# A decoder trunk whose expert search, weight splits and gate products are laid out again over the chunks of one weight stream

## The chip, the cores and the metric

One of the eight cores of a Trainium2 chip runs the whole kernel. The metric is the device time of one execution, in microseconds (us). TensorE (PE) multiplies, VectorE (DVE), ScalarE (ACT) and GpSimd (POOL) work element by element, SyncE (SP) issues transfers. Only TensorE writes products to PSUM, which has eight banks of 128 x 512 float32.

## The reference

Two layers act on `x`, 512 tokens of 1024 numbers. Each layer is a mixer (three kinds of attention) and then PEER, an expert layer, which the change is about:

```
def peer_ffn(xn, w_q, k1, k2, u, v):
    q = (xc @ w_q)                      # 8 heads, two halves of 128
    s1, s2 = q half . k1, q half . k2   # 128 scores each
    v1, i1 = lax.top_k(s1, 16);  v2, i2 = lax.top_k(s2, 16)
    cand = v1[..., :, None] + v2[..., None, :]      # 16 x 16 pairs
    top_s, top_pos = lax.top_k(cand, 16)
    ids = pair of key numbers of top_pos            # one of 128 * 128 experts
    g = jax.nn.softmax(top_s)
    act = u[ids] . xc
    y = sum over heads and 16 of  g * gelu(act) * v[ids]
```

So each token uses 8 x 16 of 16384 experts, each with a row of `u` and one of `v`.

## The kernel before, in words

All weights come as one stream of 1 MB chunks (128 x 2048 float32) through two buffers `raw[0]` and `raw[1]`. Each chunk is split for precision: ACT copies `raw` to `hi` in a rounded format (`split_hi`, L497, line L501), and DVE or POOL subtracts to get `lo` (`split_lo`, L833 on DVE with line L836; L459 on POOL with line L462). TensorE makes every product from three matmuls (`product`, L1323, lines L1325 to L1327): hi with hi, hi with lo, lo with hi. Semaphores `hi_done`, `lo_done` and `w_used` order the three: the hi split of a chunk waits until TensorE has used the chunk two before it.

PEER of a layer has these stages on TensorE:

- **Queries.** 8 chunks of `w_q`, one head each, and the key scores of that head. POOL makes the `lo` of these chunks.
- **U chunks.** 64 chunks of 256 experts. Instead of gathering rows, TensorE computes the activation of all experts for 352 of the 512 tokens: a chunk has two halves i = 0 and 1 (bank 0 and bank 1), each of 8 products, so 24 matmuls of 128x352 (`experts`, L1589). ACT applies Gelu to each bank (`gelu`, L694, lines L703 and L706), and `store_act` (L711) stores the result to DRAM.
- **Find.** Beside the first `FIND_STEPS` = 14 U chunks DVE does the search (L1081 to L1185): per head `top16` over both score halves, the candidate sums (L1106, L1108), `top16` over the candidates; then 15 rounds of a compare (L1150) and a predicated copy (L1153) over 1024 numbers that look the key numbers up. Between the rounds `low_half` makes the `lo` of chunks 9 to 14 (`LOW_HALF_AT`, L132); POOL makes that of chunks 2 to 8 in two halves (`HALVED`, line L480). In step 13 TensorE transposes the key numbers and gates of three tiles (L1611 to L1613, after waits for `idx_done` and `g_done`), and ACT evicts them (L736 to L738).
- **Gates.** For each of 352 tokens a 128 x 128 table of gates is made by one matmul of two one-hot matrices (`gates_of`, L1615, line L1623), four tokens to a group, 88 groups, one PSUM bank and one of four `onehot` slots (`G_RING`) per group. Beside each U chunk from 14 on TensorE makes three groups (`G_PER_STEP` = 3), one after half 0 and two after half 1, over 30 chunks. The one-hots of `idx1` (times the gate) are made by DVE for all groups (L1262, semaphore `oh_done`); those of `idx2` by DVE for the first group of a step (L1258) and by ACT for the other two (`OH_ACT`, `onehots`, L755: four squares, line L761, one per token, then one Relu over all four, line L764, semaphore `oh_act_done`). ACT evicts each group into `gate_s` (`g_evac`, L741, line L749) and stores eight groups as one 2 MB slice (`store_gates`, L751, line L753).
- **Tail.** The last 20 U chunks carry no gates.
- **Rows.** Tile 3 (128 tokens) and 32 tokens of tile 2 are done the sparse way: POOL gathers a row per token and rank (line L490), DVE multiplies and sums it (`row_op`, L1195; L1202 for the 32, L1204 for the 128). The 160 ops on `u` rows lie beside gates and tail.
- **V chunks.** 64 chunks; DVE multiplies activations and gates that SP loads back from DRAM (`weigh_step`), TensorE sums into all eight banks (`weighted`, L1650).

The order on each engine is written out by hand: an engine takes its instructions in order, and a wait holds all behind it. The ACT order in a gate step (L768 to L786) is what the prediction speaks of most:

```
ahead(lp + P_U + j, s)                     # hi split of the next chunk
for b in OH_ACT: onehots(...)              # two groups
gelu(0); g_evac; gelu(1); g_evac; store_act; g_evac
```

## Time and profile before

| | |
|---|---|
| median of 3 runs | 3315.04 us (3309.36 to 3315.66) |
| profiled execution | 3316.17 us |
| its span, first to last instruction | 3314.4 us |
| mean granted TensorE clock | 0.998 of 2.4 GHz |
| PE busy, DVE busy, ACT busy, POOL busy | 99%, 79%, 47%, 33% |

"Busy" is the time an engine executes. The time of an execution lies 1.8 us over its span. The two layers are alike; layer 0 ends at about 1650 us, and layer 1 repeats it some 1649 us later. The ends of matmuls are modelled, so the distance between two starts tells more than a busy share.

### The profile page before, as it was taken

The page shows a single profiled execution, that of the slowest core. Times are in us where ns is not written, and L with a number is a line of the kernel's source. Part 1 is how long each engine was busy: PE and PEld are TensorE (multiplying, and loading weights), DVE is VectorE, ACT ScalarE, POOL GpSimd, SP SyncE. Part 2 cuts the span into 40 slices and gives each one's busy share as a digit, 9 for nine tenths or more (in the row PEclk, how much of TensorE's full clock was granted, in tenths as well). Part 3 has the DMA queues.
Part 4 walks back from the last instruction along what each step waited for, and adds up shares of the span by engine and source line. Part 5 has one row for each costly group of instructions (what it writes and reads, how often), then busy time and mean ns, then how long its engine had stood idle before and what let it go on. Part 6 is the DMA issues. An engine that isn't in the chain of part 4 may idle for free. (4 is left out here: it accounts for less than half of the span.)

```text
span 3314.4 us, 55810 instructions
## 1 busy us (share of the span) xinstructions
PE 3269.3 (99%) x19734; PEld 3039.2 (92%) x19734; DVE 2610.5 (79%) x4992; ACT 1554.9 (47%) x2368; POOL 1087.6 (33%) x711
## 2 busy tenths in 40 slices
PE   8999999999999999999999999999999999999998
PEld 7767878999999999999987678789999999999998
DVE  6555448999997899999855644399999978999897
ACT  5554332467774333333355543334677733333333
POOL 1000003423335555555300000134333345555552
PEclk9999999999999999999999999999999999999999
DMA  4113322479999999999721133224899999999996
GB/s 146 62 52 115 140 104 81 171 286 383 379 383 389 420 403 411 403 409 410 284 90 64 42 124 140 103 82 176 310 379 382 378 404 416 402 409 407 404 405 251
DMA packets 230935, 894.83 MB, mean 270 GB/s; under 512 B 22784, under 2 KB 67984, under 8 KB 182912
## 3 DMA queue, kind: packets, MB, share of 16 engines
q1 hardware_dynamic: 116944, 465.34, 36.7%
q0 software_dynamic: 93008, 337.91, 26.1%
q10 hardware_dynamic: 20832, 89.74, 6.7%
q8 instruction: 72, 1.18, 0.1%
q14 instruction: 79, 0.65, 0.1%
HBM read 801.42 MB, written 91.49 MB: 269 GB/s over the span
## 5 line engine op out<-in xcount | busy, mean ns | idle before, releaser
L836 DVE TENSOR_TENSOR lo<-raw,hi 128x2048 fp32r<-128x2048 f32 (+1 forms) x320 | 728.9, 2278 | 287.4 <-ACT hi L501 284.9
L1325 PE MATMUL bank<-xT_hi,hi 128*128 128x352 f32 (+1 forms) x2688 | 928.7, 346 | 1.9 <-DVE xT_lo L886 1.7
L1326 PE MATMUL bank<-xT_lo,hi 128*128 128x352 f32 (+1 forms) x2688 | 911.5, 339 | 0.0
L1327 PE MATMUL bank<-xT_hi,lo 128*128 128x352 f32 (+1 forms) x2688 | 911.3, 339 | 0.0
L501 ACT ACTIVATE hi<-raw 128x2048 fp32r<-128x2048 f32 (+1 forms) x338 | 643.9, 1905 | 375.9 <-PE bank L1327 338.2
L1325 PE MATMUL bank<-w_hi,hi 128*128 128x352 f32 x2048 | 661.1, 323 | 0.5 <-DVE w_lo L1243 0.5
L1327 PE MATMUL bank<-w_hi,lo 128*128 128x352 f32 x2048 | 661.5, 323 | 0.0
L1326 PE MATMUL bank<-w_lo,hi 128*128 128x352 f32 x2048 | 658.1, 321 | 0.0
L1325 PEld LDWEIGHTS bank<-xT_hi,hi 128*128 128x128 f32 x2688 | 506.5, 188 | 32.3 <-issue 5.6
L490 POOL DMA_INDIRECT rows<-in_v_rows,ids x256 | 415.8, 1624 | 350.5 <-DVE h L1215 276.1
L1327 PEld LDWEIGHTS bank<-xT_hi,lo 128*128 128x128 f32 x2688 | 505.7, 188 | 26.0
L1326 PEld LDWEIGHTS bank<-xT_lo,hi 128*128 128x128 f32 x2688 | 507.2, 189 | 23.1
L490 POOL DMA_INDIRECT rows<-in_u_rows,ids x256 | 325.3, 1271 | 394.0 <-DVE act_row L1204 309.8
L1327 PEld LDWEIGHTS bank<-w_hi,lo 128*128 128x128 f32 x2048 | 386.7, 189 | 0.0
L1325 PEld LDWEIGHTS bank<-w_hi,hi 128*128 128x128 f32 x2048 | 384.4, 188 | 1.6 <-issue 1.0
L1326 PEld LDWEIGHTS bank<-w_lo,hi 128*128 128x128 f32 x2048 | 385.8, 188 | 0.0
L1215 DVE SCALAR_TENSOR_TENSOR h<-rows,w_row,h 128x1024 f32<-128x1024 f32 x256 | 327.6, 1280 | 7.3 <-DVE h L1215 1.4
L1204 DVE CUSTOM_DVE_ANT_0 rows<-rows,x_row 128x1024 f32<-128x1024 f32 x256 | 301.1, 1220 | 12.6 <-DMA rows<-in_u_rows,ids 12.6
L791 ACT ACTIVATE w_hi<-act_in 128x704 fp32r<-128x704 f32 x120 | 95.3, 794 | 392.2 <-DVE act_in L1238 392.2
L706 ACT ACTIVATE act_s<-bank 128x352 f32<-128x352 f32 x124 | 57.6, 465 | 278.3 <-PE bank L1327 278.3
L1262 DVE TENSOR_SCALAR onehot<-iota_sb,idx1T,gT 128x128 f32<-128x128 f32 x704 | 185.8, 356 | 1.0 <-ACT gT L738 1.0
L1623 PE MATMUL bank<-onehot 128*128 128x128 f32 x1408 | 176.0, 275 | 0.0
(227 smaller groups left out, 4254.1 us busy)
## 6 DMA issues: line engine op xcount, KB each, us to landing
raw<-in_stream SPq DMA_DIRECT2D x352, 1024.0 KB, 6.6
gate_d<-gate_s ACTq DMA_DIRECT2D x22, 2048.0 KB, 11.9
act_d<-act_s ACTq DMA_DIRECT2D x120, 352.0 KB, 6.4
act_in<-act_d SPq DMA_DIRECT2D x120, 352.0 KB, 7.0
gate_in<-gate_d SPq DMA_DIRECT2D x96, 384.0 KB, 9.6
gate_in<-gate_d SPq DMA_DIRECT2D x32, 256.0 KB, 4.8
rows<-in_u_rows,ids POOLq DMA_INDIRECT x256, 10.0
rows<-in_v_rows,ids POOLq DMA_INDIRECT x256, 7.5
```

What stands on the lines that cost most here:

```text
L490: pool.indirect_dma_start(rows[:, N % NR], None, a["u_rows" if n < U_ROW_OPS else "v_rows"], bass.IndirectOffsetOnAxis(which, 0)).then_inc ...
L501: act.activation(hi[s][:, 0:n], raw[s][:, 0:n], ACT.Copy).then_inc(hi_done, 1)
L706: act.activation(dst[:, s, 1, 0:TU], ps[1][:, 0:TU], ACT.Gelu).then_inc(gelu1, 1)
L791: act.activation(w_hi[:, s], acts_of(k, s), ACT.Copy).then_inc(w_hi_done, 1)
L836: dve.tensor_tensor(lo[s][:, 0:n], raw[s][:, 0:n], hi[s][:, 0:n].bitcast(F32), ALU.subtract).then_inc(lo_done, 1)
L1204: last = dve.tensor_tensor_reduce(row, row, x_row[:], 1.0, 0.0, ALU.mult, ALU.add, act_row[:, k])
L1215: last = dve.scalar_tensor_tensor(out=h[:, ROWED], in0=row, scalar=w_row[:, k], in1=h[:, ROWED], op0=ALU.mult, op1=ALU.add)
L1262: last = dve.tensor_scalar(o[:, r, 0], iota[:], idx1T[:, t], gT[:, t], ALU.is_equal, ALU.mult)
L1325: pe.matmul(dst, a_[0], b_[0], start=first, stop=False)
L1326: pe.matmul(dst, a_[0], b_[1], start=False, stop=False)
L1327: return pe.matmul(dst, a_[1], b_[0], start=False, stop=last)
L1623: last = pe.matmul(ps[4 + slot][:, tile(r)], o[:, 1], o[:, 0], start=True, stop=True)
```

## The change

`FIND_STEPS` goes from 14 to 10: the search must end four U chunks earlier. `G_PER_STEP` goes from 3 to 2: the 88 groups lie beside 44 chunks, one group after each half, and the tail shrinks from 20 chunks to 10. Of each four groups DVE makes the `idx2` one-hots of the last (`OH_DVE_AT` = 3), ACT those of the other three. Besides:

- the candidate sums move from DVE to POOL, with two buffers, and the pairs of a head are searched after the keys of the next head;
- the compare and copy of round a cover only ranks a to 15 of each 16;
- `low_half` makes the `lo` of chunks 9 and 10 alone. From chunk 11 on DVE makes the first half of each `lo`, POOL the second, between row gathers (`SHARED`, `second_half`);
- the row ops on `u` rows read their second operand from PSUM banks 2 and 3, into which ACT copies it twice per layer;
- the first V loads of gates start later (`GATES_AHEAD`), and the V blocks begin with banks 4 to 7.

The diff, cut to its core (`...` marks what is left out):

```
-FIND_STEPS = 14
-EXP_STEP, IDX_AT = 7, {13: (0, 1, 2)}
+FIND_STEPS = 10
+EXP_STEP, IDX_AT = 7, {9: (0, 1, 2)}
-G_RING, G_PER_STEP, G_TOK = 4, 3, 4
+G_RING, G_PER_STEP, G_TOK = 4, 2, 4
-V_BLOCKS = (2, 3, 4, 5, 6, 7, 0, 1)
+V_BLOCKS = (4, 5, 6, 7, 2, 3, 0, 1)
-E_GELU, E_WEIGH = 12, 14
-OH_ACT = (1, 2)
+E_GELU, E_WEIGH = 11, 13
+OH_DVE_AT = G_RING - 1
+OH_ACT = GROUPS - GROUPS // G_RING
+GATES_AHEAD = 2
...
-LOW_HALF_AT = (3, 5, 8, 10, 13)
+LOW_HALF_AT = (4,)
+CAND_AFTER = {3: 0, 4: 1, 5: 2, 7: 3, 8: 4, 9: 5, 11: 6, 12: 7}
...
@@ POOL
+                def candidates(hd):
+                    v, c = vals[:, hd % 2], cand[:, hd % 2]
+                    near, far = NEAR * TOPK, TOPK - NEAR
+                    pool.wait_ge(vals_done, PH * l + hd + 1)
+                    pool.tensor_tensor(c[:, :, 0:near]...)
+                    pool.tensor_tensor(c[:, :, near:]...).then_inc(cand_done, 1)
+                for n in range(1, C_WQ + 2):
+                    split_lo(lp + P_WQ + n // 2, n % 2)
+                    if n in CAND_AFTER:
+                        candidates(CAND_AFTER[n])
...
+                def second_half(c):
+                    s, half = c % 2, slice(HALF, CW)
+                    pool.wait_ge(lo0_done, LO0_PER_LAYER * l + len(HALVED) + c - FIND_STEPS)
+                    pool.tensor_tensor(lo[s][:, half], raw[s][:, half], hi[s][:, half].bitcast(F32),
+                                       ALU.subtract).then_inc(lo_done, 1)
+                for n in range(NR):
+                    fetch(n)
+                n = NR
+                for c in SHARED:
+                    second_half(c)
+                    while n < rows_by(c - SHARED.start) + NR:
+                        fetch(n)
+                        n += 1
@@ ACT, gate steps
                 for st in range(G_STEPS):
                     j, s = J_G + st // 2, st % 2
                     ahead(lp + P_U + j, s)
-                    for b in OH_ACT:
-                        if group(st, b) >= 0:
-                            onehots(group(st, b), OH_PER_LAYER * l + by_act(st, b))
+                    for b in range(G_PER_STEP):
+                        q = group(st, b)
+                        if q % G_RING != OH_DVE_AT:
+                            onehots(q, OH_ACT * l + by_act(q))
+                    if st == 0:
+                        act.wait_ge(e_link, 5 * l + 5)
+                        act.activation(x_in_ps, x_e, ACT.Copy).then_inc(x_ps_set, 1)
                     if st == E_GELU:
                         act.wait_ge(row_done, ROW_OPS * l + E)
+                        act.activation(x_in_ps, x_row[:], ACT.Copy).then_inc(x_ps_set, 1)
                         act.activation(w_e[:], act_e[:], ACT.Gelu).then_inc(e_gelu, 1)
                     for b in range(G_PER_STEP):
                         q = group(st, b)
-                        if b < 2:
-                            gelu(j, s, b)
-                        if q >= 0:
-                            g_evac(q)
+                        gelu(j, s, b)
+                        g_evac(q)
                         if b == 1:
                             store_act(j, s)
-                        if q >= 0 and q % PER_SLICE == PER_SLICE - 1:
+                        if q % PER_SLICE == PER_SLICE - 1:
                             store_gates(q // PER_SLICE)
@@ DVE, search
-                for hd in range(PH):
...
+                best_keys(0)
+                for hd in range(1, PH):
+                    best_keys(hd)
+                    best_pairs(hd - 1)
+                best_pairs(PH - 1)
...
-                        at[a] = looked(dve.tensor_scalar(chosen[a % 2], slot_f, float(a), None, ALU.is_equal))
+                        at[a] = looked(dve.tensor_scalar(by_rank(chosen[a % 2])[:, :, a:], by_rank(slot_f)[:, :, a:],
+                                                         float(a), None, ALU.is_equal))
...
@@ DVE, gate and tail steps
-                        if b not in OH_ACT:
+                        if q % G_RING == OH_DVE_AT:
...
-                    ahead(p, s)
+                    c = FIND_STEPS + st + 1
+                    if c in SHARED:
+                        dve.wait_ge(hi_done, 2 * (lp + P_U) + c + 1)
+                        half = slice(0, HALF)
+                        dve.tensor_tensor(lo[c % 2][:, half], ...).then_inc(lo0_done, 1)
@@ PE, gate steps
                     for i in range(2):
-                        experts(j if it is None else j + it * (G_RING // 2), s, i)
-                        for b in range(i, 2 * i + 1):
-                            q = group(st, b)
-                            if q >= 0:
-                                from_act = OH_PER_LAYER * l + 2 * ahead + by_act(st, b) if b in OH_ACT else None
-                                gates_of(l * GROUPS + G_PER_STEP * ahead + q, q % G_RING, from_act)
+                        experts(j if it is None else j + it * (G_RING // 2), s, i, shared=st > 0)
+                        gates_of(group(st, i), group(st, i) % G_RING, ahead)
```

What this does to the order of instructions is shown at three places; line numbers are those of each file (so the code of ACT's one-hots is L761 before and L807 now), `bank0` and `bank1` are the banks of the two halves, `bank4` to `bank7` those of the gate groups, and the words in brackets are the semaphores waited for.

TensorE in the second gate step, around the first group of the step; before:

```order
L1327 MATMUL bank0<-xT_hi,lo1 128x352
L1617 ISA
L1623 MATMUL bank5<-onehot 128x128 [waits g_ev,oh_done]
L1623 MATMUL bank5<-onehot 128x128 x3
L1325 MATMUL bank1<-xT_hi,hi1 128x352 [waits gelu1]
```

and now:

```order
L1394 MATMUL bank0<-xT_hi,lo1 128x352
L1686 ISA
L1688 ISA [waits oh_done]
L1692 MATMUL bank6<-onehot 128x128 [waits g_ev,oh_act_done]
L1692 MATMUL bank6<-onehot 128x128 x3
L1388 ISA
L1392 MATMUL bank1<-xT_hi,hi1 128x352 [waits gelu1,lo_done]
```

The group after half 0 waited for DVE's one-hots alone, and now waits for ACT's too (`oh_act_done`). The half behind it also waits for `lo_done` of its chunk.

ACT from the hi split of one gate step to that of the next; before:

```order
L501 ACTIVATE hi<-raw 128x2048 [waits w_used,raw_in1]
L761 ACTIVATE onehot<-iota_sb,idx2T 128x128 [waits g_ps]
L761 ACTIVATE onehot<-iota_sb,idx2T 128x128 x3
L764 ACTIVATE onehot<-onehot,one 128x4x128 [waits oh_act_link]
L761 ACTIVATE onehot<-iota_sb,idx2T 128x128 [waits g_ps]
L761 ACTIVATE onehot<-iota_sb,idx2T 128x128 x3
L764 ACTIVATE onehot<-onehot,one 128x4x128 [waits oh_act_link]
L703 ACTIVATE act_s<-bank 128x352 [waits act_out0,u0_ps]
L749 ACTIVATE gate_s<-bank 128x128x4 [waits g_ps]
L706 ACTIVATE act_s<-bank 128x352 [waits w_used]
L749 ACTIVATE gate_s<-bank 128x128x4 [waits g_ps]
L711 DMA act_d<-act_s 128x704 [waits gelu0,gelu1]
L749 ACTIVATE gate_s<-bank 128x128x4 [waits g_ps]
```

and now, in a step with an odd number (an even one has both groups' one-hots here); the last row but one stands in every fourth step:

```order
L547 ACTIVATE hi<-raw 128x2048 [waits w_used,raw_in0]
L807 ACTIVATE onehot<-iota_sb,idx2T 128x128 [waits g_ps]
L807 ACTIVATE onehot<-iota_sb,idx2T 128x128 x3
L810 ACTIVATE onehot<-onehot,one 128x4x128 [waits oh_act_link]
L749 ACTIVATE act_s<-bank 128x352 [waits act_out1,u0_ps]
L795 ACTIVATE gate_s<-bank 128x128x4 [waits g_ps]
L752 ACTIVATE act_s<-bank 128x352 [waits w_used]
L795 ACTIVATE gate_s<-bank 128x128x4 [waits g_ps]
L757 DMA act_d<-act_s 128x704 [waits gelu0,gelu1]
L799 DMA gate_d<-gate_s 128x4096 [waits g_ev]
L547 ACTIVATE hi<-raw 128x2048 [waits w_used,raw_in1]
```

The hi split stays in front of the one-hots, and the one-hots behind it are now those of the group after half 0 first.

DVE at the end of the search; before, the last rounds, with one of the five splits between rounds and the one behind them:

```order
L836 TENSOR_TENSOR lo1<-raw1,hi1 128x2048 [waits hi_done]
L1150 TENSOR_SCALAR rows<-rows 128x1024 [waits look_link]
L1153 COPY_PREDICATED rows<-rows,top_i 128x1024 [waits look_link]
L1150 TENSOR_SCALAR rows<-rows 128x1024 [waits look_link]
L1153 COPY_PREDICATED rows<-rows,top_i 128x1024 [waits look_link] x2
L836 TENSOR_TENSOR lo0<-raw0,hi0 128x2048 [waits hi_done]
L1161 TENSOR_REDUCE g_sum<-g_t 128x32 [waits exp_ready]
```

and now, from the split of chunk 9, behind which rounds 5 to 15 still stand:

```order
L1207 TENSOR_SCALAR rows<-rows 128x64x12 [waits look_link]
L1211 COPY_PREDICATED rows<-rows,top_i 128x64x13 [waits look_link]
L885 TENSOR_TENSOR lo1<-raw1,hi1 128x2048 [waits lo_done,hi_done]
L1207 TENSOR_SCALAR rows<-rows 128x64x11 [waits look_link]
L1211 COPY_PREDICATED rows<-rows,top_i 128x64x12 [waits look_link]
L1207 TENSOR_SCALAR rows<-rows 128x64x10 [waits look_link]
L1211 COPY_PREDICATED rows<-rows,top_i 128x64x11 [waits look_link]
```

Eleven compares (11 down to 1 rank wide) and twelve copies (12 down to 1) follow the split of chunk 9, then the split of chunk 10.

## Rows read from the trace of the kernel before

**Rows 1.** Windows, us: busy PE, PEld, DVE, ACT, POOL; PEclk; DMA share; GB/s.
```profile
850.00:900.00 50.00, 50.00 (x350) 50.00 (x349) 46.94 (x99) 38.92 (x79) 18.41 (x16) 1.00 0.95 371
1892.00:1902.00 10.00, 9.60 (x57) 6.32 (x57) 4.39 (x19) 5.20 (x18) 0.00 (x0) 0.83 0.01 2
```
**Rows 2.** Timeline of PE, one gate chunk and the next: start, us, operation.
```profile
807.38 0.41 PE L1325 MATMUL bank<-xT_hi,hi 128*128 128x352 f32 x1
...
811.30 1.05 PE L1623 MATMUL bank<-onehot 128*128 128x128 f32 x8
812.11 0.41 PE L1325 MATMUL bank<-xT_hi,hi 128*128 128x352 f32 x1
...
817.74 0.41 PE L1325 MATMUL bank<-xT_hi,hi 128*128 128x352 f32 x1
```
**Rows 3.** Timeline of ACT over the same chunk.
```profile
807.66 0.60 ACT L749 ACTIVATE gate_s<-bank 128x512 f32<-128x512 f32 x1 [0.30 <-PE bank L1623]
808.16 1.90 ACT L501 ACTIVATE hi<-raw 128x2048 fp32r<-128x2048 f32 x1
809.96 1.27 ACT L761 ACTIVATE onehot<-iota_sb,idx2T 128x128 f32<-128x128 f32 x4
811.26 0.72 ACT L764 ACTIVATE onehot<-onehot,one 128x512 f32<-128x512 f32 x1
...
814.16 0.59 ACT L749 ACTIVATE gate_s<-bank 128x512 f32<-128x512 f32 x1
814.78 0.34 ACTq L753 DMA_DIRECT2D gate_d<-gate_s  x1
```
**Rows 4.** Timeline of ACT, a find step: a DMA issue ahead of a split.
```profile
656.13 0.34 ACTq L711 DMA_DIRECT2D act_d<-act_s  x1
656.57 1.92 ACT L501 ACTIVATE hi<-raw 128x2048 fp32r<-128x2048 f32 x1 [0.47 <-ACT act_s L706]
```
**Rows 5.** Timeline of ACT and PE: TensorE starts on a tile of ACT's.
```profile
1891.98 0.36 ACT L611 ACTIVATE pT<-bank 128x256 f32<-128x256 f32 x1
...
1892.40 0.66 PE L1474 MATMUL bank<-pT,kv 128*64 128x128 f32 x8 [1.48 <-ACT pT L611]
```
**Rows 6.** Timeline of PE: start of U chunk 10, the transposes, chunk 14.
```profile
663.17 0.33 PE L1325 MATMUL bank<-xT_hi,hi 128*128 128x352 f32 x1
...
693.94 0.32 PE L1327 MATMUL bank<-xT_hi,lo 128*128 128x352 f32 x1
694.29 0.30 PE L1611 MATMUL bank<-ident_sb,idx_t 128*128 128x128 f32 x1
...
695.22 0.41 PE L1325 MATMUL bank<-xT_hi,hi 128*128 128x352 f32 x1
```
**Rows 7.** Timeline of DVE in the search.
```profile
641.40 0.76 DVE L1130 COPY_PREDICATED left<-qhT 128x512 uint32<-128x512 uint32 x1
642.19 2.73 DVE L1144 CAST rows<-left 128x1024 f32<-128x1024 uint32 x1
...
650.81 2.29 DVE L836 TENSOR_TENSOR lo<-raw,hi 128x2048 fp32r<-128x2048 f32 x1 [0.50 <-ACT hi L501]
653.02 0.69 DVE L1150 TENSOR_SCALAR rows<-rows 128x1024 f32<-128x1024 f32 x1
...
655.03 0.70 DVE L1150 TENSOR_SCALAR rows<-rows 128x1024 f32<-128x1024 f32 x1
655.64 1.37 DVE L1153 COPY_PREDICATED rows<-rows,top_i 128x1024 uint32<-128x1024 uint32 x1
...
689.58 2.28 DVE L836 TENSOR_TENSOR lo<-raw,hi 128x2048 fp32r<-128x2048 f32 x1
```
**Rows 8.** Timeline of ACT behind the transposes.
```profile
699.77 0.72 ACT L764 ACTIVATE onehot<-onehot,one 128x512 f32<-128x512 f32 x1
```
**Rows 9.** Groups by shape, DVE from 700 to 1010 us: busy us, mean ns.
```profile
L1262 DVE TENSOR_SCALAR onehot<-iota_sb,idx1T,gT 128x128 f32<-128x128 f32 x348 | 91.7, 355 | 0.0
L1204 DVE CUSTOM_DVE_ANT_0 rows<-rows,x_row 128x1024 f32<-128x1024 f32 x65 | 76.0, 1218 | 0.0
```

More of the change, by code:

```diff
@@ L217, in sem, with bank @@
             return ctx.enter_context(nc.semaphore(name))
-        ps = [ctx.enter_context(nc.psum_tensor(f"bank{i}", [P, T], F32)) for i in range(8)]
+        def bank(i, shape):
+            return ctx.enter_context(nc.psum_tensor(f"bank{i}", shape, F32))
+        ps = [bank(i, [P, T]) for i in range(2)]
+        x_ps_row = bank("2_3", [P, 2, T])
+        ps += [x_ps_row[:, i] for i in range(2)]
+        ps += [bank(i, [P, T]) for i in range(4, 8)]
+        x_in_ps = x_ps_row[:].rearrange("p b t -> p (b t)")
         h = sb("h", [P, NT, D])
@@ L339, in build @@
         row_gelu, row_weighed = sem("row_gelu"), sem("row_weighed")
+        x_ps_set = sem("x_ps_set")
         norm_e_in, e_link, e_gelu, e_weighed = (
@@ L481, in _, with fetch @@
                                            ALU.subtract).then_inc(lo_done if i else lo0_done, 1)
+                    if C_WQ + c in CAND_AFTER:
+                        candidates(CAND_AFTER[C_WQ + c])
                 wait_alone(pool, ids_done, 2 * l + 2, pool_passed)
-                for n in range(ROW_OPS):
+                def fetch(n):
                     N, k = ROW_OPS * l + n, n % U_ROW_OPS
@@ L1587, in _, with experts @@
                 q_steps(PH // 2 - 1, True)
-                def experts(j, s, i, first=0, end=NK, halved=None):
+                def experts(j, s, i, first=0, end=NK, halved=None, shared=False):
                     k = l * C_U + 2 * j + s
@@ L1653, in weighted @@
                     for x, d in enumerate(V_BLOCKS):
+                        if first and d == 2:
+                            pe.wait_ge(row_done, ROW_OPS * l + U_ROW_OPS)
                         if first and x >= NK - 2:
```

104 lines of the change are left out of this document (59 added, 45 removed).

## The prediction

> **What bounds the kernel now.** I read the page first, then the busy time by stretch, the waits of TensorE, and the timelines. In the gate chunks TensorE executes for the whole of each 50 us [rows 1]. The timeline tells more, since it gives starts: in U chunk 25 the first half starts at 807.38, its group at 811.30 (3.92 later), the second half at 812.11 (0.81 later), the next chunk at 817.74 [rows 2]. A chunk takes 10.36. A half and one group take 4.73; the second half and its two groups 5.63, so an adjacent group adds 0.90. That leaves 3.83 per half once the groups are out, and any group costs 0.90 wherever it stands. So TensorE sets the pace, and its work is the same after the change: 128 chunks, 176 groups. What can change the time is waiting. Spreading the groups gives nothing back, and each wait that TensorE newly meets is paid in full.
>
> **Part 1, one group after each half.** Without waits a gate chunk takes 2 x 4.73 = 9.46, and 44 chunks with two groups plus 10 without equal 30 with three plus 20 without: cost zero.
>
> The wait is on ACT. Let S be the start of a chunk. At S + 0.28 ACT starts to evict the group that ended the chunk before, at S + 0.78 it starts the hi split, at S + 2.58 the squares, at S + 3.88 the Relu, which ends at S + 4.60 (S = 807.38) [rows 3]. Before, these one-hots were for the groups after half 1, due at S + 4.73 + 3.92: ample time. Now the same order stands in the program, with two changes: the first one-hots are those of the group after half 0 (of four groups ACT makes the first three, so the group after half 0 is always ACT's), and `store_act` stands between the eviction and the split. TensorE wants the group at S + 3.92 [rows 2]; the one-hots end 0.68 later. A DMA issue holds ACT's next split 0.44 from its own start [rows 4], mostly beside the eviction (0.50 from start to start): I add 0.05. TensorE starts 0.06 after ACT's end [rows 5]; for its first matmul behind a wait I add another 0.06, most of what the first one behind a switch is longer (0.41 in [rows 2], 0.33 in [rows 6]). Together 0.85 a chunk. The loop closes: everything behind S moves with S, so nothing earns it back. The bounds are 0.68 (nothing of this shows) and 1.1 (the issue's 0.44 shows whole). In 43 chunks: 36.6 per layer.
>
> In every fourth chunk `store_gates` now stands there too. It waits for the end of the eviction and then issues (814.16 + 0.59, issue at 814.78) [rows 3]; with 0.44 from issue to split, the split starts at about S + 1.35 in place of 0.83. Ten such chunks are followed by another gate chunk: 10 x 0.54 = 5.4 per layer (bounds 3 and 6).
>
> The first gate chunk has its own order: transposes start at T, and behind them ACT's split and first one-hots end at T + 6.2 (T = 694.29) [rows 8]. TensorE starts the chunk at T + 0.93 [rows 6] and wants the group at T + 4.85. Wait: 1.5 per layer (bounds 1.3 and 2).
>
> **Part 2, the search in ten steps.** Before, T is 4.71 after the start of DVE's last `lo` split [rows 6, 7]. TensorE's last matmul ahead of them starts at 693.94 [rows 6], the next would 0.16 later: search and TensorE met within 0.2. Now the transposes are due at 663.2 [rows 6], and DVE must be 31 earlier. It sheds four splits of 2.2, the candidate sums and half of the rounds. But `lo` of chunk 9 stands behind round 4 and cannot start before 650.81, when its hi split is done [rows 7]. I expect DVE there some 5 early, and it then waits: gains ahead of that point are worth nothing.
>
> Behind it, from 653.02, the remaining work is fixed. A round took 2.01, of it 0.61 the compare and 1.40 the copy; a copy of half the size took 0.79 from start to start [rows 7]. So a copy costs 0.17 + 0.0775 per rank: twelve copies, 78 ranks, 8.1. A compare costs 0.07 + 0.033 per rank, if it keeps its rate: eleven, 66 ranks, 3.0. DVE starts the split of chunk 10 at 653.0 + 11.1 = 664.1, and T comes at 668.8. TensorE waits 5.6, before 0.2: 5.4 per layer. Bounds: 3 (copies at 0.03 fixed), and 14 (rounds of narrower operands as slow as before are 23 long; half of that excess, since the half-size row shows the fall).
>
> The compare's rate is where a rule weighs. The compare of 1024 took 0.61 from start to start, the predicated copy of as many 1.40 [rows 7]; no row has a compare on three dimensions. The Trainium skill (VectorE: DVE Perf Modes, Mode 2×_2P) says that a single-source op with both sides in SBUF handles two elements a cycle if the outermost non-unit dimension is even. It is 64 here, so by that rule the rate stays and the sum stands; were the rate halved, the 66 ranks would take 2.2 more per layer, 4.4 in all.
>
> **Part 3, the rest, costed at nothing.** The x copies on ACT (1024 wide; the 2048-wide split took 1.90 [rows 3]) lie ahead of Gelus that TensorE wants 1.5 later; the second lies in step 11. DVE per gate chunk: eight compares of at most 0.36 [rows 9], 0.3 for its share of `idx2` one-hots, half a split 1.1 [rows 7], 3.05 row ops of 1.2 [rows 9]: 8 of 10.3. If that cover goes, TensorE waits for DVE's one-hots or `lo`. POOL's halves of `lo` are due a chunk later. The last part of the first gate load is issued some two chunks before use. The V blocks' new order waits for rows that DVE ends about 2 earlier.
>
> **The sum.** Per layer 36.6 + 5.4 + 1.5 + 5.4 = 48.9; two layers 97.8. After the wait of 1.48 at 1892 TensorE's mean granted clock over 10 us was 0.83 [rows 1, 5], which is 3.4 at the lower level, 1.2 GHz, worth 1.7. I add one such fall per layer behind the wait at T: 3.4. Against the profiled execution 3316.2 + 101.2 = 3417.4; that execution lies 1.1 above the median, so **3416**.
>
> **Rivals.**
>
> *No change: the one-hots are ready in time.* If ACT took the one-hots ahead of the split, or the split ran beside the eviction, the chain from eviction to Relu (4.3) would be at most 3.6 and part 1 would cost nothing. With the search at its lower bound, 2 x 3 stays: 3322, within 0.2% of the time before. For: the four slots of one-hots free two chunks ahead. Against: the order of ACT's instructions, and the starts in [rows 3], which show no overlap. It decides at S + 3.92. Chance 0.04.
>
> *The ports.* DVE's CAST of 1024 took 2.73 where the compare of 1024 took 0.69 [rows 7]: a POOL split was running. Now POOL runs half a split in each of 53 chunks. If two of DVE's ops per gate chunk are held 2.4 each, its chunk is 8 + 4.8 = 12.8 against 10.3, and TensorE waits 88 x 2.5 = 220 more: 3636. Against: POOL's half starts when DVE's half ends, and the row ops behind it now read PSUM. The Trainium skill (SBUF — State Buffer, Who interferes with whom) has VectorE and GpSimd share one port pair as an exclusive lock, which a VectorE op takes with two SBUF inputs or in a two-port mode; by that the row ops are free of it now, and only a late half of POOL's can hold the one-hots. Chance 0.03.
>
> *The clock falls in the gate stage.* 0.85 of idle per chunk might do what 1.48 did once. One fall of 1.7 per two chunks: 44 x 1.7 = 75 more, 3491. Against: the attention stage has many waits, and the page's clock row stays at nine tenths or more in every slice. Chance 0.05.
>
> *Only the search is worse,* narrow copies no cheaper per round: 2 x 9 more, 3434. Chance 0.04, inside the range.
>
> **How the numbers follow.** Forecast 0.84. Its own range: part 1 at 0.68 gives 2 x 7.3 less, the stores and the search at their low bounds 2 x 4.8 less, no fall of the clock 3.4 less, 3388; part 1 at 1.1 gives 2 x 10.8 more, the search and stores up to 2 x 9 more, 3455. All bounds at one end at once are unlikely, so I take 3452 above; below, a further 10 covers an ACT order that overlaps more than I see. The range is 3378 to 3452; it leaves out the first three rivals and the tails. About 0.2%, some 6.6 us, is what a measurement of this kernel can tell from no change. Faster by more 0.02 (no part removes TensorE work), within 0.04, slower 0.94.
>
> **What would show it.** In the gate stage: TensorE's groups after half 0 wait for ACT's Relu, some 86 times for 0.8 to 0.9, in banks 4 and 6 alone; the chunk is 10.3 long; after the slice stores 0.5 more. At the transposes: a wait of 5 to 6 that DVE ends, with DVE idle for some 5 ahead of `lo` of chunk 9. V stage unchanged. A chunk of 9.5 in the gate stage would prove part 1 wrong; transposes near 663.5 would prove part 2 wrong; PE waits on `lo` or DVE's one-hots, the ports rival.

## The result and the profile after

The changed kernel takes 3418.57 us (median of 4 runs, 3415.62 to 3421.55) against 3313.97 for the kernel before (3309.36 to 3315.66) in the same comparison: ratio 1.0317, 95% interval 1.03 to 1.0333. That is slower by 105 us; forecast were 101. Its profiled execution took 3420.31 us, with a span of 3418.5, against 3316.17 and 3314.4.

First the window in the gate stage from [rows 1], with the columns of the rows there.

```profile
850.00:900.00 50.00, 46.41 (x305) 44.96 (x305) 33.47 (x72) 31.91 (x59) 24.52 (x19) 1.00 0.93 344
```

In the gate chunks TensorE executed for all of 50 us before, and for 46.4 now, at the full clock; all other engines have more spare time than it. The waits of TensorE, in us in all, times, longest, name what holds it:

```profile
PE bank L1692 <- ACT onehot L810: 63.9, 87, 1.4
PE bank L1680 <- DVE idx_t L1224: 13.0, 2, 6.5
PE bank L1420 <- DVE xs L924: 7.8, 1, 7.8
```

The last one stood there before as well (7.9). The first two are new: the groups wait for ACT's one-hots, and the transposes for the search. The first is short of the loss it stands for, because ends of matmuls are modelled; starts tell more. TensorE in a plain gate chunk and in one behind a store, which answers to [rows 2]:

```profile
682.10 0.41 PE L1392 MATMUL bank<-xT_hi,hi 128*128 128x352 f32 x1
...
686.79 0.38 PE L1692 MATMUL bank<-onehot 128*128 128x128 f32 x1 [0.61 <-ACT onehot L810]
...
692.44 0.41 PE L1392 MATMUL bank<-xT_hi,hi 128*128 128x352 f32 x1
...
713.15 0.41 PE L1392 MATMUL bank<-xT_hi,hi 128*128 128x352 f32 x1
...
718.39 0.38 PE L1692 MATMUL bank<-onehot 128*128 128x128 f32 x1 [1.15 <-ACT onehot L810]
...
724.06 0.41 PE L1392 MATMUL bank<-xT_hi,hi 128*128 128x352 f32 x1
...
1132.91 0.41 PE L1392 MATMUL bank<-xT_hi,hi 128*128 128x352 f32 x1
```

A chunk is 10.34 long (682.10 to 692.44; its neighbours 10.34 to 10.37) where 9.46 without a wait were expected, and 10.91 behind a store (713.15 to 724.06). ACT in those two places, as in [rows 3]:

```profile
692.72 0.60 ACT L795 ACTIVATE gate_s<-bank 128x512 f32<-128x512 f32 x1 [0.43 <-PE bank L1692]
692.81 0.34 ACTq L757 DMA_DIRECT2D act_d<-act_s  x1
693.25 1.91 ACT L547 ACTIVATE hi<-raw 128x2048 fp32r<-128x2048 f32 x1
695.06 1.27 ACT L807 ACTIVATE onehot<-iota_sb,idx2T 128x128 f32<-128x128 f32 x4
696.36 0.72 ACT L810 ACTIVATE onehot<-onehot,one 128x512 f32<-128x512 f32 x1
...
713.43 0.60 ACT L795 ACTIVATE gate_s<-bank 128x512 f32<-128x512 f32 x1 [0.43 <-PE bank L1692]
714.06 0.34 ACTq L799 DMA_DIRECT2D gate_d<-gate_s  x1
714.50 1.91 ACT L547 ACTIVATE hi<-raw 128x2048 fp32r<-128x2048 f32 x1 [0.47 <-ACT gate_s L795]
```

From S = 692.44 the Relu ends at S + 4.64; forecast were S + 4.65, against a wish of S + 3.92. Behind a store the split starts at S + 1.35, as forecast. And the search, DVE and then TensorE:

```profile
650.61 2.29 DVE L885 TENSOR_TENSOR lo<-raw,hi 128x2048 fp32r<-128x2048 f32 x1 [3.14 <-ACT hi L547]
652.82 0.52 DVE L1207 TENSOR_SCALAR rows<-rows 128x704 f32<-128x704 f32 x1
653.26 1.03 DVE L1211 COPY_PREDICATED rows<-rows,top_i 128x768 uint32<-128x768 uint32 x1
...
657.63 1.03 DVE L1211 COPY_PREDICATED rows<-rows,top_i 128x576 uint32<-128x576 uint32 x1
...
661.95 0.72 DVE L1211 COPY_PREDICATED rows<-rows,top_i 128x320 uint32<-128x320 uint32 x1
...
662.88 0.43 DVE L1211 COPY_PREDICATED rows<-rows,top_i 128x256 uint32<-128x256 uint32 x1
...
664.75 2.37 DVE L885 TENSOR_TENSOR lo<-raw,hi 128x2048 fp32r<-128x2048 f32 x1
```
```profile
669.55 0.45 PE L1680 MATMUL bank<-ident_sb,idx_t 128*128 128x128 f32 x1 [6.51 <-DVE idx_t L1224]
...
676.36 0.33 PE L1394 MATMUL bank<-xT_hi,lo 128*128 128x352 f32 x1
676.52 1.06 PE L1692 MATMUL bank<-onehot 128*128 128x128 f32 x8
```

The window from 664 to 680 us (busy PE, PEld, DVE, ACT, POOL; clock) shows what the granted clock did behind that wait. Before, it was 1.00 there.

```profile
664.00:680.00 16.00, 10.45 (x58) 10.45 (x58) 14.50 (x39) 8.10 (x21) 6.14 (x6) 0.79 0.59 195
```

A clock of 0.79 leaves out 0.21 of 16 us; at half the clock that is 6.7 us at 1.2 GHz. The trace's record of the clock has the fall from 667.3 to 674.1, 6.8 us, and one of the same length in layer 1.

**The account.** In layer 0 the gate stage runs from 671.36 to 1132.91, 461.55 us, where 44 x 9.46 = 416.2 would do: 45.3 a layer, 90.6 in all. The wait at the transposes is 6.3 longer than before in each layer, 12.6. From the transposes to chunk 10 it takes 1.81 in place of 0.93 at the lower clock, 1.8 for both. Sum 105.0; the spans differ by 104.1. Of the 45.3, 1.24 belong to the first even group (676.52, which is 5.16 behind the start of its chunk and not 3.92). In layer 0 it waits for nothing: it starts 0.16 behind the matmul before it, and the half in front of it was long because its first nine matmuls ran at the lower clock. In layer 1 it waits 0.38.

### The profile page after: what moved, and what is told of

Read it like the earlier page. It is cut to its first block and busy times, and to the rows that moved or that the text cites. A ratio compares the mean times of both kernels' runs of the same rounds, so it can differ in the third digit from the quotient of the medians.

```text
span 3418.5 us, 56118 instructions
## 1 busy us (share of the span) xinstructions
PE 3296.8 (96%) x19734; PEld 3041.5 (89%) x19734; DVE 2461.6 (72%) x4946; ACT 1585.4 (46%) x2442; POOL 1265.1 (37%) x849
## 5 line engine op out<-in xcount | busy, mean ns | idle before, releaser
L885 DVE TENSOR_TENSOR lo<-raw,hi 128x2048 fp32r<-128x2048 f32 (+1 forms) x214 | 486.4, 2273 | 196.4 <-ACT hi L547 193.3
L518 POOL DMA_INDIRECT rows<-in_v_rows,ids x256 | 416.2, 1626 | 352.0 <-DVE h L1276 277.4
L525 POOL TENSOR_TENSOR lo<-raw,hi 128x1024 fp32r<-128x1024 f32 x106 | 253.2, 2389 | 417.4 <-DVE lo L1327 417.3
L1327 DVE TENSOR_TENSOR lo<-raw,hi 128x1024 fp32r<-128x1024 f32 x106 | 129.9, 1225 | 350.2 <-ACT hi L547 350.1
L1265 DVE CUSTOM_DVE_ANT_0 rows<-rows,bank 128x1024 f32<-128x1024 f32 x256 | 298.5, 1216 | 0.0
L518 POOL DMA_INDIRECT rows<-in_u_rows,ids x256 | 244.2, 954 | 68.3 <-issue 58.8
L1692 PE MATMUL bank<-onehot 128*128 128x128 f32 x1408 | 194.5, 281 | 63.9 <-ACT onehot L810 63.9
## 6 DMA issues: line engine op xcount, KB each, us to landing
gate_d<-gate_s ACTq DMA_DIRECT2D x22, 2048.0 KB, 12.4
```

The lines of the kernel that those rows point to most:

```text
L518: pool.indirect_dma_start(rows[:, N % NR], None, a["u_rows" if n < U_ROW_OPS else "v_rows"], bass.IndirectOffsetOnAxis(which, 0)).then_inc ...
L525: pool.tensor_tensor(lo[s][:, half], raw[s][:, half], hi[s][:, half].bitcast(F32), ALU.subtract).then_inc(lo_done, 1)
L885: dve.tensor_tensor(lo[s][:, 0:n], raw[s][:, 0:n], hi[s][:, 0:n].bitcast(F32), ALU.subtract).then_inc(lo_done, 1)
L1265: last = dve.tensor_tensor_reduce(row, row, x_in_ps, 1.0, 0.0, ALU.mult, ALU.add, act_row[:, k])
L1327: dve.tensor_tensor(lo[c % 2][:, half], raw[c % 2][:, half], hi[c % 2][:, half].bitcast(F32), ALU.subtract).then_inc(lo0_done, 1)
L1692: last = pe.matmul(ps[4 + slot][:, tile(r)], o[:, 1], o[:, 0], start=True, stop=True)
```

## The experiments

The kernel before was run again beside each run. Its median moved between 3314 and 3318 us from one comparison to the next, so I compare ratios to it; one thousandth is 3.3 us. Theory A: the even groups, those behind half 0, wait for ACT, about 90; the search costs the rest.

### ACT's order, the first one-hots ahead of the split

```
@@ ACT, gate step
-                    ahead(lp + P_U + j, s)
                     for b in range(G_PER_STEP):
                         q = group(st, b)
                         if q % G_RING != OH_DVE_AT:
                             onehots(q, ...)
+                        if b == 0:
+                            ahead(lp + P_U + j, s)
```


> ScalarE makes each step's first one-hots before it starts the hi part of the next chunk, and the hi part after them; nothing else is changed. Theory A (the changed kernel's +104 us is some 90 us of even groups that wait for ScalarE's one-hots, because the PSUM copy and the hi part stand in front of them, and some 14 us of the search): the first one-hots are ready some 2.8 us after the half-chunk boundary, wanted at 3.9, so the waits before even groups, the 0.6 us more in chunks that store and the first 1.2 us vanish: 3418.6 - 90 = 3328 us (3324 to 3340), and the wait of the split for the hi part grows by 1.8 us without harm. Rival P (the ports that VectorE and GpSimd share): GpSimd's half is late, so a hi part that comes 1.8 us later makes the chunk's second half later still: slower than 3418.6, by up to 1 us in each of 86 chunks. Rival C (the clock or the weight transfers, 340 GB/s now against 380): the time stays within 10 us of 3418.6. Rival S (the search alone): stays at 3418.6.

Measured: 3336.97, ratio 1.0066 (1.005 to 1.0083): 83 us of the 105 are gone. Every gate chunk behind the first is 9.46 long by the starts of its groups. The 1.2 at the first even group, which was to go too, stayed: the group starts 7.0 and 6.7 behind the transposes without a wait, as the lower clock lets it.

### The first one-hots a step earlier

```
-                        if q % G_RING != OH_DVE_AT:
+                        if q % G_RING != OH_DVE_AT and (st == 0 or b > 0):
                             onehots(q, ...)
...
                         g_evac(q)
+                        if b == 0 and st < G_STEPS - 1:
+                            onehots(q + 2, ...)
```


> ScalarE makes the first one-hots of a step one step earlier, in the time in which it waits for the previous step's second half-chunk; the hi part stays where it is. Theory A: the even groups' one-hots are there several us early, and the hi part is not delayed: 3328 us (3322 to 3335), the same as with the exchanged order or up to 3 us less. If the exchange is worse than this by more than 5 us, the delay of the hi part has a price of its own (split, GpSimd's half). Rivals C and S: within 10 us of 3418.6.

Measured: 3334.72, ratio 1.0058 (1.0041 to 1.0075), 86 us less than the change. ACT and then TensorE in this kernel:

```profile
748.66 0.60 ACT L795 ACTIVATE gate_s<-bank 128x512 f32<-128x512 f32 x1 [0.43 <-PE bank L1694]
...
749.29 0.75 ACTq L799 DMA_DIRECT2D gate_d<-gate_s  x1
750.14 1.91 ACT L547 ACTIVATE hi<-raw 128x2048 fp32r<-128x2048 f32 x1 [0.89 <-ACT gate_s L795]
...
754.71 1.28 ACT L807 ACTIVATE onehot<-iota_sb,idx2T 128x128 f32<-128x128 f32 x4
756.02 0.72 ACT L810 ACTIVATE onehot<-onehot,one 128x512 f32<-128x512 f32 x1
```
```profile
757.03 1.05 PE L1694 MATMUL bank<-onehot 128*128 128x128 f32 x8
761.76 1.05 PE L1694 MATMUL bank<-onehot 128*128 128x128 f32 x8
```

The one-hots of the even group at 761.76 are ready at 756.74, five us early. The groups come every 4.73. Even a store whose issue takes 0.75 costs nothing here. The work is the same, only one block of ACT's instructions moved, so the cause of 86 us is shown: ACT's order. Rival C (the clock or the transfers) and rival S (the search) are refuted as the cause of this part, and so is P (the ports) by the exchange, which came out faster and not slower. Exchange and step ahead differ by less than their intervals.

### Another ring place for DVE

```
-OH_DVE_AT = G_RING - 1
+OH_DVE_AT = 0
...
-    return q - q // G_RING + 1
+    return q - q // G_RING
```


> VectorE makes the one-hots of ring place 0 in place of 3; ScalarE makes those of 1, 2 and 3, still three quarters. Theory A: half of the even groups are then VectorE's, which has its share ready several us early, and the stores of gates fall in just those chunks: per layer 22 x 0.89 (the loss of an ordinary chunk) + 10 x 0.57 + 1.24 = 26.5 us less, 53 for two layers: 3366 us (3358 to 3374). Rival P: the same work for VectorE and GpSimd, so no change. Rival T (ScalarE is simply too busy with three quarters, wherever they lie): no change either, or a wait before odd groups in its place.

Measured: 3372.32, ratio 1.017 (1.0153 to 1.0187), 49 us less; 53 were expected. TensorE waits 44 times for ACT's one-hots, not 87:

```profile
PE bank L1692 <- ACT onehot L810: 27.9, 44, 1.1
```

Half of the even groups are DVE's, and half of the loss went, and the store's surcharge with it. ACT's amount of work is unchanged, so rival T (too much work for ACT) is out. The chunks alternate between 9.57 to 9.60 and 10.24: the short ones are 0.1 longer than without a wait, the long ones 0.1 shorter than in the change, which about cancels. What is missing to 53 is mostly the 1.2 a layer at the first even group. That group is DVE's here and waits for nothing, yet it starts 7.6 and 7.1 behind the transposes, 7.0 and 6.9 in the change: what holds it is the lower clock, not ACT. (The clock fell for 10.2 us in layer 0 here, for 6.8 in layer 1.)

### One more activation in front

```
+                    if q % 2 == 0 and q > 0:
+                        act.activation(spare[:], iota[:].unsqueeze(1).to_broadcast([P, 3, P]), ACT.Copy)
                     for r in range(G_TOK):
```


> One more ScalarE activation of 128x384 (some 0.5 us from one start to the next) in front of the one-hots of every even group but the first two; nothing reads what it writes. Theory A (ScalarE's chain from the evacuation through the hi part and the one-hots to the even group sets the length of every gate chunk): each of 86 chunks grows by all of it: 3418.6 + 43 = 3462 us (3450 to 3475). Rival C (clock, transfers) or rival S (the search): ScalarE is idle half of the time, and the time stays within 5 us of 3418.6.

Measured: 3468.46, ratio 1.0461 (1.0443 to 1.0478), 48 us more than the change.

```profile
752.22 0.51 ACT L807 ACTIVATE spare<-iota_sb 128x384 f32<-128x384 f32 x1
752.63 1.27 ACT L810 ACTIVATE onehot<-iota_sb,idx2T 128x128 f32<-128x128 f32 x4
```

The added activation takes 0.41 from its start to the next, and a plain chunk grew from 10.34 to 10.37 to 10.75 to 10.79. That is theory A's dose: 3462 was expected. From the first even group to the last, the gate stage of layer 0 is 22.7 longer (473.5 against 450.7): 43 x 0.41 = 17.6, three chunks that took 1.3 to 1.5 more each, and 0.6 in the first. Layer 1 has three such chunks too. In the one of these that I followed ACT waited 1.75 for the odd group where 0.43 is usual; TensorE's starts show no delay. What held it is open. In four of the six, which stand in two pairs, there is more: TensorE waited 2.3 for the even group between the two, and there the granted clock fell for 3.4 us (at 1039.6 and at 2469.8); a like wait at 743.9 brought no fall. So the rival of a falling clock in the gate stage is not out of reach; in the change itself, with waits of at most 1.4, it did not come.

### The low half of chunk 9 two rounds later

```
-LOW_HALF_AT = (4,)
+LOW_HALF_AT = (6,)
```


> The low half of the one chunk that VectorE splits within its search is moved from after round 4 to after round 6 of 15, so that the 3.1 us in which VectorE waits for that chunk's hi part are used by two rounds of copies. Theory S (the search is late by what VectorE waited there): the search ends some 3 us earlier in each layer, the wait of TensorE for its results falls from 6.5 to 3.5 us, and the stretch at half clock that follows becomes shorter or vanishes: 6 to 13 us less, 3405 to 3412. Rival: the copies are slow for want of the ports that GpSimd holds, so that the rounds moved forward take longer and nothing is won: 3418.6 +- 3. If the low half of the chunk is late for TensorE instead: slower by up to 3 us a layer.

Measured: 3421.38, ratio 1.032 (1.0303 to 1.0337): no difference from the change. But the wait did shrink, and the clock stayed at 1.00 in the window from 664 to 680 us (in layer 1 it fell for 3.4 us):

```profile
PE bank L1692 <- ACT onehot L810: 70.8, 88, 1.3
...
PE bank L1680 <- DVE idx_t L1224: 7.0, 2, 3.5
```

So 6 us came off one wait, and 7 went onto the other. From the first even group to the last the gate stages of the two layers took 453.9 and 453.3, against 450.7 and 451.0: a dozen chunks of each are 0.2 longer than their neighbours (10.56 for 10.35). The odd group's eviction starts 1.2 to 1.3 behind the group's start in them, 1.09 elsewhere. I know where the gain went, not why. With no fall of the clock in layer 0, the first even group starts 6.26 behind the transposes, after a wait of 1.24 for ACT's one-hots; in the change it takes 6.97. So the fall of 6.8 us costs 0.7 net there. The next run takes ACT's chain away.

### Both edits

> Both edits together: ScalarE makes a step's first one-hots one step earlier, and the low half is moved from after round 4 to after round 6. Moving the low half alone brought TensorE's wait for the search from 6.5 to 3.5 us and the stretch at half clock behind it away in one layer, yet won nothing, while the waits before even groups grew by 7 us. Theory G (what the search won was lost again in the chain of ScalarE that sets the gate stage): with that chain gone, the gain shows: 2 x 2.8 us of the wait and 2 to 4 us of the clock for each layer at full speed again: 3334.7 - 6 to - 12 = 3323 to 3329 us. Rival N (the search never was on the path that sets the end): 3334.7 +- 2, as the first-one-hots edit alone.

Measured: 3324.81, ratio 1.0037 (1.0023 to 1.005), 7 us under the first-one-hots edit alone (1.0058). All gate chunks are 9.46. The waits at the transposes are 3.5, as without the first edit. Theory G fits, with 3323 to 3329 expected: the search is on the path, and with ACT's chain gone its gain shows.

### Find stage of 12 chunks

```
-FIND_STEPS = 10
+FIND_STEPS = 12
...
-LOW_HALF_AT = (4,)
+LOW_HALF_AT = (6, 11, 16)
```
(on top of the one-hots a step earlier)

> The edit of the one-hots (one step earlier) and a find stage of 12 chunks in place of 10, its low halves after rounds 6, 11 and 16. If the rest of the loss is the search that ends 6.5 us after TensorE's chunks, two more chunks (15.4 us) cover it: no wait at the transposes, no fall of the clock behind it, 2 x (6.5 + 1.7 to 3.4) = 16 to 20 us less than 3334.7: 3315 to 3319, that is level with the kernel before (3317 in the last comparison). If two more splits in the search make it late again, or the tail of 8 chunks is too short for VectorE's row operations, a wait comes back and the time stays at 3320 to 3335.

Measured: 3326.65, ratio 1.003 (1.0019 to 1.0042): no wait at the transposes and no fall of the clock there, as expected, but not the 16 to 20 us. The waits that came in its place:

```profile
PE bank L1394 <- DVE w_lo L1306: 6.1, 6, 1.9
...
PE bank L1394 <- DVE lo L1329: 4.6, 5, 1.3
```
```profile
1135.94 1.23 DVE L1329 TENSOR_TENSOR lo<-raw,hi 128x1024 fp32r<-128x1024 f32 x1 [4.63 <-ACT hi L547]
```

```profile
1133.99 1.91 ACT L547 ACTIVATE hi<-raw 128x2048 fp32r<-128x2048 f32 x1 [5.69 <-DMA raw<-in_stream]
```

`lo` is late in the tail although DVE stood idle for 4.63 in front of it: the `hi` was late, and in front of that ACT had waited 5.69 for the weight chunk. From 1085 to 1250 us ACT's splits waited 24.6 for such transfers in all, and 9.2 in the kernel with both edits and a find stage of 10. So the weight chunks came late. Why is open: the DMA share from 1090 to 1150 us was 0.99, and 1.02 to 1.03 in that kernel and in the kernel before, where TensorE had no wait for `lo` in the tail.

### Who splits which chunk

Three runs, each with the one-hots a step earlier. First more halves for GpSimd, up to chunk 10; the split at the end of the search, `next_chunk = low_half()`, is taken out too. A second run gives it chunk 9 alone, `range(2, 10)`, and keeps that split:

```
-HALVED = range(2, 9)
+HALVED = range(2, 11)
-LOW_HALF_AT = (4,)
+LOW_HALF_AT = ()
```


> The edit of the one-hots (one step earlier), and GpSimd splits chunks 9 and 10 of the find stage too, in halves as it does 2 to 8, so that VectorE's search holds no split at all; find stage of 10 chunks as in the changed kernel. Theory S (what is left over the kernel before, 8 us after both edits, is the search: the wait of 3.5 us per layer and the clock behind it): the search loses two splits of 2.3 us and its last wait for a hi part, against up to two VectorE operations held up by some 2 us behind GpSimd's halves: the wait at the transposes falls from 3.5 to 0 to 2 us, no fall of the clock: 3324.8 - 6 to - 12 = 3313 to 3319 us, level with the kernel before (3315.7). Rival L (GpSimd's halves hold up as much of the search as they take off it): 3322 to 3330.

> The same with chunk 9 alone given to GpSimd; VectorE splits chunk 10 at the end of the search. Theory S: one split of 2.3 us and a wait of 0.4 us less in the search than with the low half after round 6, up to 2 us more held up: the wait at the transposes is 1 to 3.5 us, 3318 to 3325 us. Rival L: 3325 to 3330. In both cases the version that also gives away chunk 10 is faster by the 2.3 us twice if nothing is held up.

Measured: 3337.7, ratio 1.0061 (1.0048 to 1.0075), and 3327.77, ratio 1.0041 (1.0027 to 1.0055). Both missed the range of theory S; the first also lies above rival L's 3322 to 3330, the second inside it. With no split left in the search it became not shorter: TensorE waits 7.1 and 6.7 at the transposes, and 5.3 and 5.1 with chunk 9 alone given away, where both edits together had 3.5. So each chunk given to GpSimd made the search some 1.7 later. GpSimd's own halves are the reason. POOL and DVE of the first of the two:

```profile
647.77 5.88 POOL L507 TENSOR_TENSOR lo<-raw,hi 128x1024 fp32r<-128x1024 f32 x2 [1.98 <-ACT hi L767]
```
```profile
647.49 1.32 DVE L1213 COPY_PREDICATED rows<-rows,top_i 128x832 uint32<-128x832 uint32 x1
648.84 2.54 DVE L1209 TENSOR_SCALAR rows<-rows 128x704 f32<-128x704 f32 x1
651.30 3.25 DVE L1213 COPY_PREDICATED rows<-rows,top_i 128x768 uint32<-128x768 uint32 x1
```

The same compare of 704 took 0.52 and the same copy of 768 took 1.03 in the change; here they take 2.54 and 3.25, and each such row falls on one half of POOL's (the POOL row holds two, back to back). A half costs the search 2.0 to 2.2, a chunk up to 4.4; VectorE does the whole chunk in 2.3. My theory S had the sign wrong. So the other way round:

```
-HALVED = range(2, 9)
+HALVED = range(2, 7)
-LOW_HALF_AT = (4,)
+LOW_HALF_AT = (2, 5, 9)
```


> The opposite of the last two: the edit of the one-hots (one step earlier), and VectorE takes the splits of chunks 7 and 8 from GpSimd, after rounds 2 and 5 of its search, that of chunk 9 after round 9, that of chunk 10 at the end. Theory L (each half of a split on GpSimd holds up one VectorE operation of the search by some 2.2 us, so a chunk given to GpSimd costs the search 4.4 us, and one that VectorE splits itself 2.3): two chunks taken back win 2 x 2.1 us, and the rounds moved ahead of the splits fill the waits for the hi parts: the search ends some 4 us earlier than in the version with the low half after round 6 (its wait at the transposes was 3.5 us), the wait goes to 0 to 1 us and no fall of the clock is left: 3324.8 - 8 to - 11 = 3314 to 3317 us, level with the kernel before (3315.9). Rival S (what counts is the number of splits in the search): two splits more make the search 4.6 us later, a wait of 8 us, 3335 to 3342.

Measured: 3320.3, ratio 1.0008 (0.9999 to 1.0017). The search holds two more splits than the change's and ends earlier:

```profile
644.49 2.29 DVE L887 TENSOR_TENSOR lo<-raw,hi 128x2048 fp32r<-128x2048 f32 x1 [0.38 <-ACT hi L547]
...
659.95 2.29 DVE L887 TENSOR_TENSOR lo<-raw,hi 128x2048 fp32r<-128x2048 f32 x1
```
```profile
664.68 0.30 PE L1682 MATMUL bank<-ident_sb,idx_t 128*128 128x128 f32 x1
...
670.93 1.16 PE L1694 MATMUL bank<-onehot 128*128 128x128 f32 x8 [1.22 <-ACT onehot L810]
```

The transposes start without a wait, and no fall of the clock follows. Here the first even group does wait for ACT, 1.22, since its one-hots can't be made a step ahead. Those 1.2 a layer fit the 2.7 us that the ratio gives, though its interval (0 to 5.6 us) would fit much else. The 3320.3 lie above the 3314 to 3317 expected; the kernel before stood at 3318.1 in this comparison, not at 3315.9. Spread groups with these two repairs are level with the kernel before; none of these versions beat it.

### x from SBUF again

```
-  ... tensor_tensor_reduce(row, row, x_in_ps, ..., act_e[:, n:n + 1])
+  ... tensor_tensor_reduce(row, row, x_e, ..., act_e[:, n:n + 1])
-  ... tensor_tensor_reduce(row, row, x_in_ps, ..., act_row[:, k])
+  ... tensor_tensor_reduce(row, row, x_row[:], ..., act_row[:, k])
```


> The row operations of the up stage read x from SBUF again, as before the change; all else is the changed kernel (the copies of x to PSUM are still made). Theory A: they lie in VectorE's spare time (3.6 us idle before each half split), so the time stays at 3418.6 +- 3. Rival P (VectorE and GpSimd are bound to each other by their ports, and the PSUM operand relieves it): with both operands in SBUF GpSimd's halves and fetches are held up again, the fetch goes back from 0.95 to 1.2 us and the half of 2.4 us grows; if that is on the path, slower by 10 us or more.

Measured: 3440.92, ratio 1.0377 (1.036 to 1.0394), 20 us more than the change. I had expected nothing; rival P had 10 or more. POOL from 700 to 1000 us (busy, mean ns, idle), DVE and ACT of this kernel:

```profile
L525 POOL TENSOR_TENSOR lo<-raw,hi 128x1024 fp32r<-128x1024 f32 x29 | 94.9, 3271 | 79.3 <-DVE lo L1327 78.9 <-issue 0.4
L518 POOL DMA_INDIRECT rows<-in_u_rows,ids_e x22 | 28.6, 1300 | 5.6 <-issue 5.3
```
```profile
752.28 3.40 DVE L1263 CUSTOM_DVE_ANT_0 rows<-rows 128x1024 f32<-128x1024 f32 x1
```
```profile
758.49 0.71 ACTq L799 DMA_DIRECT2D gate_d<-gate_s  x1
759.31 1.91 ACT L547 ACTIVATE hi<-raw 128x2048 fp32r<-128x2048 f32 x1 [0.84 <-ACT gate_s L795]
```

In the change a half takes POOL 2.38, a fetch 0.95, a row op DVE 1.22. With both operands in SBUF a half takes 3.27, a fetch 1.30, and one row op in a chunk 3.4, the others 1.22. The Trainium skill (SBUF — State Buffer, Who interferes with whom) says that a VectorE instruction with two SBUF inputs contends with a GpSimd one that reads SBUF, and one with a single SBUF input outside the two-port modes doesn't; the trace agrees on both. What made the kernel longer is less clear. A chunk behind a store went from 10.9 to 11.24 to 11.47, since the issue of the store took 0.71 for 0.34 ahead of the split; the plain ones stayed at 10.34 to 10.38, but for one of 10.75, so the halves and row ops that take longer cost TensorE nothing there. The two gate stages are 4.2 and 4.6 longer. The stretches from the last gate matmul to the first product of the V stage are 2.8 and 4.7 longer (79.7 and 82.1 against 76.9 and 77.4), and TensorE's waits for `w_lo` grew from 0.9 to 4.4 in all. The first even group of layer 0 comes 2.0 later. That is 18.3 of the 18.7 between the two profiled executions. But the next run shows that the long issue doesn't come with x in SBUF.

> The edit of the one-hots (one step earlier) with x read from SBUF again. On top of the changed kernel x from SBUF cost 20 us: the chunks that store gates grew from 10.9 to 11.3 us (the issue of the store took 0.71 us in place of 0.34), and more was lost where the V stage begins. Theory A2 (the store's issue costs only because it stands in ScalarE's chain ahead of the even group): with one-hots made a step ahead the gate stage keeps its 9.46 us per chunk, and only the loss at the V stage stays: 3334.7 + 5 to + 14 = 3340 to 3349 us. Rival P (VectorE and GpSimd hold each other up so that halves come late for TensorE, whatever ScalarE does): the gate chunks are longer than 9.46 us and the time is over 3350.

The same edit on top of the one-hots a step earlier measured 3337.8, ratio 1.0071 (1.0056 to 1.0087), against 1.0058 without it: 4 us more, which lies inside the intervals, and a little under the 3340 to 3349 expected. The gate chunks stay at 9.46, though POOL's halves take 3.19: rival P, in which late halves hold TensorE, is refuted for the gate stage. It is no test of theory A2, for the gate stores' issues took 0.34 here, all 22, while x came from SBUF as well. In the three runs on who splits which chunk they took 0.66 to 1.01, all 22, and there x was in PSUM. So the 8.8 us of the gate stages in the first run went through ACT's chain, but that x in SBUF caused them is not shown.

## Why the prediction was right, point by point

**Part 1, chain of ACT.** Forecast 0.85 a chunk; by starts it is 0.88 to 0.91 (10.34 to 10.37 against 9.46), with the Relu at S + 4.64. The rule "same order, new first customer" was right, and the exchange and the ring place show it as cause, not only as timing. **The store** cost 0.57 for 0.54. **The first chunk** cost 1.24 for 1.5, but in layer 0 that is the lower clock and not the forecast's wait: the group waited for nothing. Together the three are 45.3 a layer for 43.5. That the term of the first chunk comes out near its forecast is luck. The forecast's cost of zero for the spread itself is right, though its sentence that takes 44 chunks with two groups and 10 without as equal to 30 with three and 20 without leaves out the four chunks that came over from the find stage (7.66 each) and counts two groups too many.

**Part 2, the search.** Forecast a wait of 5.6; 6.5 was measured. DVE idled 3.1, not 5, before `lo` of chunk 9. That changed nothing, as the text had it. The remaining work was forecast at 11.1 and took 11.9 (652.82 to 664.75), and the copies are where it went: 8.9 for 8.1. The forecast drew a straight line through two widths, 512 and 1024, and a copy doesn't follow it. From start to start, those of 768 to 576 took 1.06 to 1.11, those of 512 to 320 took 0.73 to 0.75, those of 256 to 128 took 0.47: the price steps at each 256 numbers, four ranks. On the line 768 would be 1.10 and 320 would be 0.56. The compare kept its rate: 704 took 0.44 from start to start, so the doubled price, against which the rule of the Trainium skill (VectorE: DVE Perf Modes, Mode 2×_2P) spoke, did not come. The upper bound of 14 was not what its sentence says: half of the excess of 12.4 over 5.4 gives 11.6.

**The clock.** Here a term was missized in both directions. The fall lasts 6.8 us and not 3.4 in each layer. In layer 0, 2.3 of it lie beside the wait, 1.8 under the transposes, which cost 0.88, and 2.7 under the first half, which cost 1.24. The forecast had 1.7 for the clock and, as a second term, 1.5 for ACT's one-hots in the same stretch. The two overlap: together they cost 2.1 in place of 3.2, and with no fall 1.4 would be left (6.26 behind the transposes against 4.85).

**Part 3, costed at nothing.** In the change as it stands it holds: in the gate stage TensorE waits for nothing but ACT's one-hots. With x from SBUF the kernel is 20 us slower, but the gate chunks without a store kept their length, so the row ops' cover held there. The argument never looked at ACT's DMA issue, whose length costs as soon as something due stands behind it.

**Rivals.** No change: refuted, ACT's operations do not overlap enough. Ports as the bound: refuted for the forecast's place (DVE idles 3 to 4 us in each gate chunk, and its one-hots are never late), but the mechanism is real, in the search and wherever both inputs lie in SBUF. Clock in the gate stage: 1.00 from 680 to 1100 us; only the kernel with the added activation had such falls, two of 3.4 us. Search alone: with the clock behind it, it is one seventh of the loss.

## What to carry to other kernels

When a step is moved to an earlier place in a loop, ask of each engine that feeds it which of its instructions stand in front of the feeding one, and count from the last thing that released them; here one-hots 0.7 us too late in a chunk of 9.5, and 0.5 more behind a store, cost some 86 us. A buffer ring with free places is worth nothing if the engine that fills it does so late in its own order: fill it in the step before, where that engine idles. And a helper engine isn't free help: compare what it takes off with what it holds up on the engine it shares ports with.

## What the runs showed that I had not expected

- A predicated copy on VectorE is held by GpSimd as compares and casts are: copies of 640 to 960 numbers took 1.0 to 1.4 us alone and 3.2 to 3.6 where a half of a split runs on GpSimd. In the kernel before, the copies took at most 1.4, and the rows showed it of the cast alone [rows 7].
- The price of a predicated copy steps with each 256 numbers: 0.47 us from start to start at 256, 0.75 at 320 and at 512, 1.06 at 576 and at 768. Of four ranks of 64 numbers that are left out one after the other, only one makes the copy shorter.
- Waits of 6.4 to 7.1 us at the transposes brought a fall of the clock of 6.8 us in 13 of 16 layers of the profiled kernels and one of 10.2 in the other three; waits of 5.3 and 5.1 us brought 6.8 and 3.4; waits of 3.5 us brought 3.4 in three of four and none in one, where 1.5 had been followed by 3.4 [rows 1, 5].
- The issue of a gate store by ACT took 0.34 in 21 of 22 cases of the change (once 0.61). With x from SBUF it took 0.67 to 0.90 in all 22, and with x from SBUF and the one-hots a step earlier 0.34 in all 22; other versions have both. What decides between the two is open; it costs nothing unless something due stands behind it.
- Shortening a wait ahead of a stage that one engine's chain paces gave nothing at all, not even the time up to the stage: chunks grew by 0.2 here and there. What sets those 0.2 is open.
